# Activations' and weights' buffers start at nine relative positions within 256 bytes

## The reference, cut to what matters

```python
def layer_ab(x, norm_g, w_in, ...):
    h = rms_norm(x, norm_g)
    g_q, g_k, g_v, ... = jnp.split(h @ w_in, split_idx, axis=-1)
    ...
    return x + jnp.concatenate([o_gla, o_fox], axis=-1) @ w_out
def layer_c(...):
    u, gate = jnp.split(h @ w_in, 2, axis=-1)
    ...
    z = z * jax.nn.sigmoid(z @ glu_w + glu_b)
    return x + (z * jax.nn.silu(gate)) @ w_out
```

## Time and profile before

| What | Value |
|---|---|
| median of three runs | 3286.36 us |
| profiled execution, first to last instruction (span) | 3282.2 us |
| PE busy | 3260.7 us (99%), 15570 matmuls |
| PEld busy | 2654.6 us (81%) |
| DVE busy | 2089.5 us (64%) |
| ACT busy | 1269.9 us (39%) |
| POOL busy | 140.0 us (4%) |
| granted PE clock, mean | 0.999 |

### The profile page before, as it was taken

One profiled execution on the slowest core, in us unless ns is written; L12 is line 12 of the kernel. 1 busy time (PEld: TensorE's weight loads), 2 busy tenths in 40 slices (PEclk: granted clock), 3 DMA queues, 4 the chain that ended last, 5 costly groups with the idle time before them and its releaser, 6 DMA issues.

```text
span 3282.2 us, 42519 instructions
## 1 busy us (share of the span) xinstructions
PE 3260.7 (99%) x15570; PEld 2654.6 (81%) x15570; DVE 2089.5 (64%) x3172; ACT 1269.9 (39%) x1987; POOL 140.0 (4%) x116
## 2 busy tenths in 40 slices
PE   8999999999999999999999999999999999999999
PEld 7888888787888888888888887787778888778777
DVE  5665657687766565634354676687757477676863
ACT  4333324444443344523232224624534222642641
POOL 3000000001020000000020000000003000000000
PEclk9999999999999999999999999999999999999999
DMA  5433436677776666756443454545557353555445
GB/s 181 129 118 104 142 122 203 216 243 258 268 261 208 189 207 191 240 185 212 148 169 122 145 165 156 186 145 177 178 174 254 112 170 130 188 166 179 169 162 205
DMA packets 302095, 588.80 MB, mean 179 GB/s; under 512 B 64280, under 2 KB 111128, under 8 KB 301888
## 3 DMA queue, kind: packets, MB, share of 16 engines
q1 hardware_dynamic: 301888, 586.09, 53.8%
HBM read 453.77 MB, written 132.20 MB: 179 GB/s over the span
## 4 chain that ended last, share of the span: by engine, by line
PE 94%; DVE 3%; ACT 1%; DMA 1%; DVEq 1%; issue 1%; SPq 0%; ACTq 0%
PE bank L560 70%; PE bank L559 13%; PE bank L2012 1%; PE bank L1596 1%; PE bank L1101 1%; PE bank L737 1%; PE bank L1131 1%; PE bank L1452 1%; PE bank L1421 1%; PE bank L2333 1%; PE bank L1608 0%; PE bank L1006 0%; PE bank L2363 0%; PE bank L1610 0%; DVEq L2643 0%
## 5 line engine op out<-in xcount | busy, mean ns | idle before, releaser
L560 PE MATMUL bank<-act_high,weights_high 128*128 128x512 f32 x3584 | 1422.3, 397 | 12.5 <-DVE act_low L543 10.8
L560 PE MATMUL bank<-act_low,weights_high 128*128 128x512 f32 x3584 | 1399.6, 391 | 0.0
L472 DVE TENSOR_TENSOR weights_low<-weights_raw,weights_high 128x1024 fp32r<-128x1024 f32 x528 | 655.8, 1243 | 717.0 <-ACT weights_high L403 704.1
L403 ACT ACTIVATE weights_high<-weights_raw 128x1024 fp32r<-128x1024 f32 x528 | 557.7, 1057 | 1407.3 <-PE bank L560 1198.6
L560 PE MATMUL bank<-act_high,weights_low 128*128 128x512 f32 x3584 | 963.0, 389 | 0.0
L560 PEld LDWEIGHTS bank<-act_high,weights_high 128*128 128x128 f32 x3584 | 674.8, 188 | 161.0 <-DVE act_low L543 10.8
L560 PEld LDWEIGHTS bank<-act_high,weights_low 128*128 128x128 f32 x3584 | 672.8, 188 | 139.8
L560 PEld LDWEIGHTS bank<-act_low,weights_high 128*128 128x128 f32 x3584 | 675.1, 188 | 135.9 <-issue 1.2
L559 PE MATMUL bank<-weights_high,act_high 128*128 128x512 f32 x640 | 253.1, 396 | 0.0
L559 PE MATMUL bank<-weights_high,act_low 128*128 128x512 f32 x640 | 249.4, 390 | 0.0
L2110 DVE SCALAR_TENSOR_TENSOR residual_in<-residual_in,arena 128x512 f32<-128x512 f32 x240 | 181.2, 755 | 20.6 <-issue 2.0
(11 more groups left out here) (323 smaller groups left out, 2514.8 us busy)
## 6 DMA issues: line engine op xcount, KB each, us to landing
weights_raw<-in_w_all SPq DMA_DIRECT2D x528, 512.0 KB, 3.5
convert_in<-mix SPq DMA_DIRECT2D x80, 256.0 KB, 4.6
fm_b<-stream_out SPq DMA_DIRECT2D x72, 256.0 KB, 3.3
mix<-arena SPq DMA_DIRECT2D x64, 256.0 KB, 3.1
x_part<-stream_out SPq DMA_DIRECT2D x48, 256.0 KB, 4.6
residual_in<-x_part SPq DMA_DIRECT2D x48, 256.0 KB, 5.2
x<-stream_out SPq DMA_DIRECT2D x48, 256.0 KB, 5.2
convert_in<-x SPq DMA_DIRECT2D x48, 256.0 KB, 4.0
```

Source lines behind the costliest of these rows:

```text
L403: e.activation(WH[:, t % 3, :], RAW[:, t % 3, :], ACT.Copy).then_inc(wh_ready, 1)
L472: e.tensor_tensor(WL[:, t % 3, :], RAW[:, t % 3, :], WH[:, t % 3, :].bitcast(F32), ALU.subtract).then_inc(wl_ready, 1)
L560: return e.matmul(bank[s][:, :], a[:, s * P:(s + 1) * P], h, start=start, stop=stop)
```

## The change

Two fillers of 128 bytes are put ahead of act_high and act_low. weights_high and weights_low become one tensor each with 256 bytes more, and their three buffers begin 144, 4272 and 8400 bytes into it (high) and 160, 4288 and 8432 bytes (low). The arena is shortened by 192 elements, 768 bytes, the sum of what is added. In the diff, offsets count elements of four bytes.

```diff
+        sb("before_act_high", [P, 32])
         HH = sb("act_high", [P, KT, L], F32R)
+        sb("before_act_low", [P, 32])
         HL = sb("act_low", [P, KT, L], F32R)
         RAW = sb("weights_raw", [P, 3, 2 * L])
-        WH = sb("weights_high", [P, 3, 2 * L], F32R)
-        WL = sb("weights_low", [P, 3, 2 * L], F32R)
+        WH_ALL = sb("weights_high", [P, 6 * L + 64], F32R)
+        WL_ALL = sb("weights_low", [P, 6 * L + 64], F32R)
+        WH = [WH_ALL[:, at:at + 2 * L] for at in (36, 1068, 2100)]
+        WL = [WL_ALL[:, at:at + 2 * L] for at in (40, 1072, 2108)]
...
-        ARENA_N = 20032
+        ARENA_N = 19840
...
-            e.activation(WH[:, t % 3, :], RAW[:, t % 3, :], ACT.Copy).then_inc(wh_ready, 1)
+            e.activation(WH[t % 3], RAW[:, t % 3, :], ACT.Copy).then_inc(wh_ready, 1)
...
-            e.tensor_tensor(WL[:, t % 3, :], RAW[:, t % 3, :], WH[:, t % 3, :].bitcast(F32), ALU.subtract
+            e.tensor_tensor(WL[t % 3], RAW[:, t % 3, :], WH[t % 3].bitcast(F32), ALU.subtract
                             ).then_inc(wl_ready, 1)
...
-                a = (WL if part == 2 else WH)[:, b, k * L:(k + 1) * L]
+                a = (WL if part == 2 else WH)[b][:, k * L:(k + 1) * L]
```

## The result

The changed kernel takes 3338.83 us (3336.77 to 3339.97, four runs) against 3286.25 us (four runs of the kernel before), a ratio of 1.0158 (95% interval 1.0146 to 1.0171), or 52.6 us more. The forecast was 3347 us.

The account below looks back on a forecast made before the run. PE was taken to bound the kernel; 4.8 ns more on each of 12672 products gave 61 us, all other terms about 0, so 3282.2 + 61 = 3343 us of span, 3347 us with 4.2 us to the median; range 3255 to 3390 us.

Parts of the forecast that it names:

- PE bounds the kernel, nothing covers a product: Whole kernel: PE busy 99% of the span, so every nanosecond on each of 12672 products is 12.7 us.
- The term of the positions: Large projections: unequal operand positions raise each product from 227.7 to 232.5 ns, 61 us over 12672 products.
- L737 is slow for its position: Small products at L737: 234.2 ns each because their operands lie 96 bytes apart, 7.5 ns over the long stretches.
- Equal positions fall into step, L737's never do: fp32r products: at equal positions load and stream reach a repeating step costing 13.4 ns; at 96 bytes they never do.
- 64 bytes may behave as equal: One of the nine relative positions, 64 bytes, may cost the same as equal ones; the mean hardly moves.
- Distances that differ by t % 3 and by part: Long stretch: start-to-start times would differ between units by t % 3, and between parts 0 and 1 and part 2.
- L737's act_low products as before: Small products at L737: those with act_low, still 96 bytes apart, keep their times; act_high ones possibly change.
- Conversions 0, fillers and transfers 0: ACT's and DVE's conversions keep 1057 and 1243 ns; fillers, shorter arena and transfers add nothing; 0 us.
- Restart 0: First product after token mixing, 340 ns: its load stands alone with no stream beside it, so 0 change.
- Rival A: All products: positions do nothing, L737's 7.5 ns come from its single bank or place; 3286 us, chance 0.17.
- Rival B: Projections: unequal positions are better, products fall towards 216 ns; 3237 us with one in three, 3138 with all; chance 0.14.
- C and D: Projections: C, some lengthen, some fall in step, 3303 to 3315 us, 0.10; D, all worse than L737, 3369 to 3442, 0.07.

Follow-up runs that it names:

- e9: Kernel before with activations at 144 within 256 bytes, weights at 240 where stationary and at 0 where moving; 3296.45 us, ratio 1.0033.
- e4: Kernel before with small_weights moved to start at 128 within 256 bytes, at distance 0 from act_high and act_low; 3284.14 us, one run.
- e2: Kernel before with weights 0 to 112 bytes after activations (at 128), seven units each, in the long stretch only; 3293.9 us, one run.
- the surveys: Four kernels trying many weight distances by groups of units, activations at 128 (3293.9, 3291.36 us), 144 (3331.84 us) and 0 (3301.92 us).
- e1: Kernel before with act_high, act_low and all six weight buffers starting 16 bytes later, distance 0 kept; 3330.08 us, ratio 1.0136.
- e10: Kernel before with activations at 144 within 256 bytes, weights at 168 where stationary and at 208 elsewhere; 3321.25 us, ratio 1.0109.
- e11: Kernel before, activations at 128; in the long stretch, weight distances such as 96, 16, 240 and 0 follow each other in groups of four units; 3301.94 us.
- e12: Kernel before with small_weights at distance 0, plus extra small products with 64 or 32 stationary columns, or 256 moving columns; 3303.12 us, one run.

## Why the prediction was right, point by point

- *PE bounds the kernel, nothing covers a product:* right. 54.9 us on the products, 54.0 us on the span.
- *The term of the positions,* 4.8 ns x 12672 = 61 us: right in sign, a little large. I had 227.7 ns now and 232.5 after; measured are 227.3 and 231.8, 4.5 ns on the 12140 products that are followed by another within 260 ns, 55 us. In the long stretch it is 5.0 ns (I said 324 us, it is 322.5). My 228.8 ns for 120 products was misread: those 27.46 us hold a second slow start in the middle (distances of 279 and 335 ns in a row, then ten slow ones), not one alone.
- *That the size came out is partly luck.* 232.5 was put between two neighbouring rows by a mechanism that is wrong (below), not worked out for these nine distances. Single pairs ran at 226.7 to 236.7 ns. e9 has no equal positions either, and the same reasoning would have said 61 us for it; it took 11 us more than the kernel before.
- *L737 is slow for its position:* right, shown by e4 (226.8 ns at distance 0) and e2 (234.3 ns in another part of the kernel at distance 96).
- *Equal positions fall into step, L737's never do:* wrong as a mechanism. All places in the surveys fall into a repeating pattern. Many that cost more are just as regular, e1's 232 and 228 ns for one. Distance 0 isn't enough (e1, 230.0 ns). What the kernel before has is one of a few fast patterns, and from 128 and from 0 it is reached at distance 0 from every state that these runs passed through.
- *64 bytes may behave as equal:* wrong, 233.3 ns.
- *Distances that differ by t % 3 and by part:* right, but small. In the long stretch parts 0 and 1 take 231.1, 231.4 and 231.8 ns for t % 3 = 0, 1 and 2, and part 2 takes 232.9, 232.6 and 232.0.
- *L737's act_low products as before:* wrong, 230.0 ns for both. The pattern belongs to the sequence, not to one product.
- *Conversions 0, fillers and transfers 0:* right. *Restart 0:* right, the first of the products after other work, 245 in all, has its next one after 331.2 ns where it was 331.6. The reason I gave for it was not tested.
- *Rival A (positions do nothing)* fell with the result. I had drawn it from the two independent ports that the Trainium skill, TensorE: Matmul & The Clock Gate, "Step-by-step: what each phase is for", gives TensorE. That conclusion, that the start of an operand is free, does not hold: 226.7 against 231.7 ns in the long stretch. Whether the ports themselves ever meet, no run here shows.
- *Rival B (better elsewhere)* fell in the surveys: over fifty pairs and none settled below 226.7 ns. *C and D* fell by the mean of 231.8 ns.

Open: what in the chip makes the pattern. The runs show that places, the size of the load and the past choose it, and no more. The traces speak against one rival, the traffic of the other engines. ACT's and DVE's conversions come once in 24 products, and the bank changes from tile to tile, yet in the long stretch of e1 232 and 228 ns alternate within 1 ns through nearly 1400 products, and the kernel before keeps 227, 227, 226 ns there just as evenly.

## What to carry to other kernels

Where fp32r products run back to back, read the distance from start to start in ns: 226.7 or 233.3 ns is a 3% difference on the product, and whole kernels lost 0.3% (e9) to 1.6% here. Moving all operands by 16 bytes was enough for 1.4% (e1). Keep stationary and moving operands at the same multiple of 128 bytes within 256: it came back to 226.7 ns from every state here and in both roles of the weights (of the unequal pairs tried in whole kernels, only e10's with moving weights did so in all of its 80 units). And watch small buffers ahead of large ones that shift them. Measure such a thing in the whole kernel, since a survey's value for a pair of places holds only for the state in which it was entered.

## What the runs showed of the hardware that I had not expected

- The same products at the same places run at 226.7 or 233.4 ns, by what ran before them (e11), and keep that to the end of their group.
- In each pattern short enough to be read off, the length is a whole multiple of 6.67 ns, 16 cycles at 2.4 GHz: 226.67 (34 of them), 460 for two products (69), 473.3 for two (71), 687 for three (103), 913.3 for four (137), 1640 for seven (246), and 120 with 256 moving columns (18).
- Fewer stationary columns can slow a product: 230.0 ns with 64 and 231.6 with 32, 226.7 with 128 at the same points of the program (e12 and e4).
- The conversions of ACT and DVE take 1057 and 1241 ns at the starts of the change and of e1, multiples of 16 bytes, where they took 1057 and 1243 ns at multiples of 128.
